# Block attention on one core: when a head's value products are issued

## The reference, cut to what matters

```python
def moba_attention(q, k, v, rel_bias):      # MOBA_BLOCK = 256 = S
    ...
    logit_own = jnp.einsum('bhqd,bhkd->bhqk', qc, k_own).astype(jnp.float32) + bias_own[None]
    logit_own = jnp.where(dist_own >= 0, logit_own, NEG_INF)
    p = jax.nn.softmax(jnp.concatenate([logit_sel, logit_own], axis=-1), axis=-1)
    ...
def second_block(...):
    y_a = (from_heads(ret) * jax.nn.silu(rg)) @ ret_w_branch[l]
    att = moba_attention(mq, mk, to_heads(mv, MOBA_HEADS), rel_bias)
    y_b = from_heads(att) @ moba_w_branch[l]
    merged = jax.nn.sigmoid(ga) * y_a + jax.nn.sigmoid(gb) * y_b
```

## Time and profile before

| | |
|---|---|
| median of 3 runs | 1862.27 us |
| span of the profiled execution | 1856.2 us |
| TensorE busy | 1790.4 us (96%) |
| VectorE busy | 1275.7 us (69%) |
| ScalarE busy | 889.7 us (48%) |
| GpSimd busy | 1004.1 us (54%) |
| attention stage, first scores to first retention output unit | 918.11 to 973.53 us |
| TensorE busy in that stage | 50.67 of 55.42 us |
| granted TensorE clock in that stage | 1.00 |

### The profile page before, as it was taken

One profiled execution on the slowest core, in us unless ns is written; L12 is line 12 of the kernel. 1 busy time (PEld: TensorE's weight loads), 2 busy tenths in 40 slices (PEclk: granted clock), 3 DMA queues, 4 the chain that ended last, 5 costly groups with the idle time before them and its releaser, 6 DMA issues.

```text
span 1856.2 us, 31003 instructions
## 1 busy us (share of the span) xinstructions
PE 1790.4 (96%) x10878; PEld 1537.8 (83%) x10878; DVE 1275.7 (69%) x2158; ACT 889.7 (48%) x1507; POOL 1004.1 (54%) x431
## 2 busy tenths in 40 slices
PE   5999899998999999999999999999999999999999
PEld 1847579897988887788869799999999988888887
DVE  6587757888547877424233369988999957777776
ACT  3034545444436554542444546655655555555554
POOL 4033146443666543685427778877776754444443
PEclk7999999999999999999999999999999999999999
DMA  8787236876564554553315455554444455555555
GB/s 322 251 304 251 89 128 237 277 279 203 189 233 166 191 192 161 182 169 115 121 69 162 163 175 182 182 164 164 160 159 157 151 182 192 192 192 192 192 193 169
DMA packets 95323, 346.02 MB, mean 186 GB/s; under 512 B 10544, under 2 KB 12032, under 8 KB 94592
## 3 DMA queue, kind: packets, MB, share of 16 engines
q1 hardware_dynamic: 78048, 283.67, 45.4%
q10 hardware_dynamic: 17184, 61.11, 9.4%
HBM read 343.66 MB, written 1.08 MB: 186 GB/s over the span
## 4 chain that ended last, share of the span: by engine, by line
PE 70%; DVE 14%; issue 6%; POOL 4%; DMA 3%; ACT 2%; DVEq 0%; ACTq 0%; POOLq 0%; SPq 0%
PE ps L624 26%; PE ps L559 19%; PE ps L571 5%; POOL ring_lo L504 4%; PE ps L577 3%; PE ps L780 2%; PE ps L543 2%; DMA ring<-stream 2%; PE ps L847 2%; PE ps L694 2%; PE ps L1010 2%; PE ps L794 1%; DVE arena L2768 1%; DVE ps L2765 1%; DMA cst<-consts 1%
## 5 line engine op out<-in xcount | busy, mean ns | idle before, releaser
L504 POOL TENSOR_TENSOR ring_lo<-ring,ring_hi 128x1024 fp32r<-128x1024 f32 x371 | 901.1, 2434 | 662.6 <-ACT ring_hi L498 661.2
L498 ACT ACTIVATE ring_hi<-ring 128x1024 fp32r<-128x1024 f32 x502 | 531.7, 1060 | 500.1 <-DMA ring<-stream 497.4
L559 PE MATMUL ps<-h_span,ring_hi 128*128 128x256 f32 x3296 | 431.8, 284 | 0.0
L559 PEld LDWEIGHTS ps<-h_span,ring_hi 128*128 128x128 f32 x3296 | 411.4, 191 | 5.4 <-issue 3.3
L624 PE MATMUL ps<-ring_hi,e_pair 128*128 128x512 f32 x1024 | 253.7, 389 | 0.9 <-DVE e_pair L2796 0.9
L2796 DVE TENSOR_TENSOR e_pair<-arena,e_pair 128x256 fp32r<-128x256 f32 x128 | 174.6, 1365 | 99.3 <-ACT e_pair L1821 98.9
L559 PE MATMUL ps<-h_span,ring_lo 128*128 128x256 f32 x1648 | 231.4, 283 | 0.8 <-POOL ring_lo L504 0.7
L624 PEld LDWEIGHTS ps<-ring_hi,e_pair 128*128 128x128 f32 x1024 | 192.1, 188 | 41.1 <-issue 1.3
L559 PEld LDWEIGHTS ps<-h_span,ring_lo 128*128 128x128 f32 x1648 | 212.5, 192 | 1.5 <-POOL ring_lo L504 1.5
L504 DVE TENSOR_TENSOR ring_lo<-ring,ring_hi 128x1024 fp32r<-128x1024 f32 x141 | 178.6, 1268 | 37.0 <-ACT ring_hi L498 36.8
L624 PE MATMUL ps<-ring_hi,arena_r 128*128 128x512 f32 x672 | 176.4, 395 | 3.6 <-ACT ring_hi L498 3.6
(11 more groups left out here) (301 smaller groups left out, 2298.2 us busy)
## 6 DMA issues: line engine op xcount, KB each, us to landing
ring<-stream SPq DMA_DIRECT2D x540, 512.0 KB, 3.3
arena<-aside_w ACTq DMA_DIRECT2D x49, 512.0 KB, 4.8
late<-aside_w ACTq DMA_DIRECT2D x21, 512.0 KB, 4.7
resid<-aside_w ACTq DMA_DIRECT2D x10, 512.0 KB, 6.7
arena<-scale_w ACTq DMA_DIRECT2D x8, 512.0 KB, 15.2
arena<-ln_rows ACTq DMA_DIRECT2D x8, 512.0 KB, 5.3
arena<-gate_cols ACTq DMA_DIRECT2D x2, 1024.0 KB, 4.9
arena<-decay ACTq DMA_DIRECT2D x1, 1536.0 KB, 6.8
```

The costliest lines, as they stand in the source:

```text
L498: act.activation(ring_hi[:, s, :], ring[:, s, :], ACT.Copy).then_inc(hi_ready, 1)
L504: eng.tensor_tensor(ring_lo[:, s, :], ring[:, s, :], ring_hi[:, s, :], ALU.subtract).then_inc(lo_ready[s], 1)
L559: m = pe.matmul(ps[:, bank, 0:T], w[:, kc * P:(kc + 1) * P], x[:, kc, :], start=begin, stop=w is w_lo and kc == KC - 1)
```

## The change

The values of head h are issued in step 2h + 4 instead of 2h + 3: in an even step, behind the scores and ahead of the gate unit. They wait for the copies of the two maps of their own head (counts kept when the maps are turned), not for all fills of banks 4 and 5. The loop ends at step 16, and the values of the last head are issued behind the first of the retention's eight output units. An argument that nobody used (`late_part`) goes. Only TensorE's program is changed.

```diff
-            def attention(n_maps, scores, keys_of, at_t, values, early=None, late_part=None):
-
-                for m in range(n_maps + 2):
+            def attention(n_maps, scores, keys_of, at_t, values, early=None):
+
+                turned = {}
+                for m in range(n_maps + 1):
                     if m < n_maps:
                         scores(m)
+                    if m >= 4 and m % 2 == 0:
+                        values(m // 2 - 2, *(turned[m - k] for k in (4, 3)))
                     if early is not None:
                         early(m)
-                    if m >= 3 and m % 2 == 1:
-                        pe.wait_ge(emptied[4], fills[4].now())
-                        pe.wait_ge(emptied[5], fills[5].now())
-                        values(m // 2 - 1)
                     if 1 <= m <= n_maps:
...
                         fills[b].add()
-                    if late_part is not None:
-                        late_part(m)
+                        turned[k] = fills[b].n
+                return turned[n_maps - 2], turned[n_maps - 1]
...
-            def values_m(hd):
+            def values_m(hd, even_turned, odd_turned):
                 jt, g = divmod(hd, 2)
                 b = 6 + jt % 2
+                pe.wait_ge(emptied[4], even_turned)
+                pe.wait_ge(emptied[5], odd_turned)
...
-            attention(16, scores_m, lambda k: k % 2 + 1, lambda k, kt: m_attn[:, k % 2, kt * P:(kt + 1) * P],
+            last_turned = attention(16, scores_m, lambda k: k % 2 + 1, lambda k, kt: m_attn[:, k % 2, kt * P:(kt + 1) * P],
...
                 parts_tile(split_unit(u), ret_hi, ret_lo, lambda kc: kc * P, 4 + n % 2, u, True)
+                if n == 0:
+                    values_m(7, *last_turned)
```

## The result

The changed kernel takes 1872.14 us (median of 6 runs, 1871.12 to 1874.28), the kernel before 1861.61 us beside it (6 runs, 1859.35 to 1866.18): 1.005 times as long, interval 1.0031 to 1.0069. So it is slower, by about 10 us where I forecast 2, and outside my range. In a second comparison it was 1869.94 against 1864.57 us, ratio 1.0047 (1.0028 to 1.0066).

The account below looks back on a forecast made before the run. In the block attention TensorE was taken as the bound, working without pause except 4.8 us of waits. +3.50 us in the loop and -1.38 at the end gave +2.12, so 1864.4 us, range 1861.5 to 1867.4.

Parts of the forecast that it names:

- part (a): Values leave odd maps 3 to 11; the transpose comes 2.30 instead of 2.56 us after the scores: -1.30 us.
- part (b): Six heads' values enter even maps 4 to 14, where no pause hides them: +4.80 us (3.9 to 5.4).
- part (c): From the scores of map 15, the second output unit comes at 8.16 instead of 9.54 us: -1.38 us.
- the rival I gave 12%: Pauses at odd maps 3 to 15 make the clock fall, 1.5 us each: 1867.4 us and more; chance 0.12.
- The sum and its base: Whole kernel: +2.12 us on the 1856.2 us span, plus an unchanged 6.1 us around it: 1864.4 us.
- My spread of 1.5 us: Whole kernel: 1.5 us added either side of a median, from earlier runs at 1860.2 to 1863.0 us.
- The faster rival: Odd maps: the gate wait is the true bound, so removing it gives -4.4 us, 1857.9 us; chance 0.08.
- The shift carries to the end: Behind the second output unit: later stages start from TensorE's results, so the +2.12 us reaches the kernel's end.

Follow-up runs that it names:

- e_drain: The kernel before, with ScalarE draining the gate unit ahead of rounding a weight unit in the even maps: 0.9996 of the kernel before (0.9982 to 1.001).

## Why the prediction was wrong

I forecast +2.1 us: +3.5 in the loop, -1.4 at the end, nothing for the clock. The runs show +4.7, +0.3 and +1.4, 6.4 us in all. So three steps failed: the price of the values at even maps, the credit at the end, and the clock's term that I put at nothing. What is left of the 10.5 us of the first comparison is dealt with under the sum.

- **Waits at the odd maps, part (a): right.** 2.30 us at each, the pause released by VectorE's normalisation, the last at 0.97 us. `e_drain` confirms the -0.26 us a head: its transposes come 2.30 us behind the scores at all the odd maps.
- **Price of the values at even maps, part (b): mis-sized.** 0.98 us instead of 0.80, above my upper end of 0.9, six times: 1.1 us more. I took it from map 3, where an idle time stood in front. From the values to the gate unit it is 0.79 us (937.49 to 938.28), as I had it; but the values start 0.42 us after the scores' last pair, where the gate unit had started after 0.24. I read the instruction's cost at its end and not at both its borders. Loop: +4.7 us, forecast +3.5.
- **The end, part (c): wrong.** I credited 1.38 us. I had modelled the end after the change at full clock well (8.16 us, measured 8.35; the terms as I wrote them add up to 8.10, since 8/24 of 2.95 us is 0.98 and not 1.04), but subtracted it from an end of before that held a fall. At full clock before takes 8.05 us, so the part costs 0.3. All of the credit was the fall's, and falls come and go.
- **The clock inside the loop, put at nothing: the rival I gave 12% is what happens.** One fall at map 1 hadn't occurred in one trace, and I let that one row speak for seven pauses; in another trace of the same order it did occur there. The price of 1.5 us for each was right. The changed kernel had 8 falls in five traces, 1.6 each, 2.4 us; the kernel before 2 in three traces, 1.0 us. The net is 1.4 us, so this alone would not have taken the time out of my range. Here the Trainium skill ("TensorE: Matmul & The Clock Gate", section "A second HAM failure mode: psum-queue depth-cycling") was on the right side, and the trace agrees: frequent pauses of 0.97 us, falls; the same loop with them filled, none.
- **The sum and its base.** 4.7 + 0.3 + 1.4 = 6.4 us. By medians the three comparisons gave 10.5, 5.4 and 7.5 us, and 6.4 lies inside the intervals of the first two (5.8 to 12.8 and 5.2 to 12.3 us). What the first has above 6.4 can be chance, though no run shows it directly: six runs of a kernel whose runs lie 12.7 us apart, and a profile with 5.8 us of falls ahead of the stage, which the kernel before can have as well. Which falls its other five runs had isn't on record. With 6.4 us and the median that I started from, 1862.27, the time would have been 1868.7, outside my range too. My spread of 1.5 us came from three runs; 31 runs spread over 16 us. I also took 6.1 us as lying around the span; in the changed kernel's runs it is 2.1, and the rest was the luck of the profiled execution of before.
- **The faster rival** fell: `e_drain` takes the gate wait away and gains 1.3 us, not 2.2.
- **"The shift carries to the end": right.** Behind the second output unit the two kernels take the same time, within what their own traces differ.

## What to carry to other kernels

When a wait is removed from an in-order engine, measure the next one from the same origin: the second releaser here let the transpose go only 0.26 us sooner than the first, and the work moved out of the pause cost 0.98 us where it landed. Work that stands in a wait costs nothing extra; before moving it, look whether the wait can be shortened at its source, which here were two swaps of order on other engines. Subtract only stretches at the same clock, and count its falls in several traces before one of them is booked as gain or loss. One row without a fall doesn't show that a pause is safe.

## What I had not expected of the hardware

The unchanged kernel differs by up to 16 us from run to run on one core (1857.47 to 1873.82), and part of it is the clock. Of the 31 runs, the four with a mean granted clock of 0.986 have a median of 1868.4 us, the four with 0.990 one of 1860.1. Two traces show stays at 1.2 GHz at 264, 441, 561 and 974 us in the one and at 204, 265, 559, 828, 897 and 1852 us in the other (leaving out the first 50 us), each 3.4 or 6.8 us long. The clock fell at rows of small products (8 of 15 traces at one, 13 of 15 at the other) and behind pauses of 0.97 us in otherwise dense work (10 falls in the loop, each 0.7 to 1.6 us behind such a pause's end), in some executions and not in others; it did not fall behind the loop's pauses of 0.43 us in four traces, nor behind those of 0.32 us in three.
